# Ten modulation steps of the first FFN: from 32-column matmuls to weighted sums on VectorE

## The chip, the cores and the metric

One core of one Trainium2 chip. The metric is the device time of one launch in microseconds (us); the kernel before took 1458.21 us, the median of three runs.

## The reference

Two transformer blocks of width 1024 on 256 tokens, all in float32. What matters here is the modulation of the first block: from the condition vector c come 6 vectors of 1024 for each layer and 2 for the keys and values, and they shift, scale and gate the activations.

```python
c_act = jax.nn.silu(c)
for l in range(DEPTH):
    shift1, scale1, gate1, shift2, scale2, gate2 = jnp.split(c_act @ ada_w[l] + ada_b[l], 6, axis=-1)
    if l == N_A_LAYERS:
        k_shift, k_scale = jnp.split(c_act @ kv_ada_w + kv_ada_b, 2, axis=-1)
...
    h = modulate(rms_norm(x, norm2_g[l]), shift2, scale2)
    x = x + gate2[:, None, :] * swiglu(h, ffn_w_gate[l], ffn_w_up[l], ffn_w_down[l])
```

So each product is one row of 1024 numbers times a 1024 x 512 block of weights (2 MB), 28 such blocks in all.

## The kernel before

The kernel streams all weights once from HBM. Each engine has its program written out by hand, and semaphores alone tie them; SyncE's queue issues the weight loads in the order in which they will be used.

**The weight stream.** A unit is a block of weights in a ring of four slots (RING): eight k-tiles by 256 columns (1 MB) for gate and up matrices, five or six k-tiles by 256 for the down matrix (DOWN_K, line 40). `take` (line 386) loads unit u when unit u-4 is done (`unit_done`). For the FFNs each unit is split in two parts of reduced width, so that three fast matmuls stand for one of float32: ScalarE casts it (`w_high`, line 594, into PARTS), VectorE subtracts (`w_low`, line 1022, into WL), and TensorE runs the triple in `mm3` (line 1642). All TensorE rows carry line 1610, the helper `mm`.

**The first FFN** (`ffn(0)` in each engine's program; `silu_ffn(0)` on ScalarE). The hidden width of 2816 goes in MT = 11 pairs, each a gate unit and an up unit: 96 matmuls of 128x256 (`gate_up`, line 1719). Behind each pair ScalarE takes the silu (line 614), VectorE multiplies (line 1043), ScalarE and VectorE split the product (lines 625, 1064), and between these they split the next units. Then come the down matrix's 16 units d0 to d15 in four column groups c (`down`, line 1772), 132 matmuls a group. The first group needs the hidden parts; groups 2 and 3 need the two PSUM banks that VectorE read in `down_used` (line 1081), where it also adds the residual and makes the low parts of the units from d4 on.

**The ten modulation steps within it.** 28 blocks of modulation weights are handled as steps s; ten of them (ADA_FFN0, line 42; steps 10 to 19) are done in this FFN, beside its weights. Their loads don't use the ring but an area of their own, ADW, with two halves of 256 columns (`ada_load`, line 396). A step is done by TensorE in two stages:
- `ada_rows` (line 1662), ahead of each pair from the second on: for each of the two halves and eight k-tiles one matmul with 32 copies of the activation CACT as weights. The k-tiles go to four groups of 32 PSUM rows, so that the result is four partial sums in four bands of rows.
- ScalarE copies them to ROWS (`row_copy`, line 684), which has two buffers, s % 2.
- `ada_cols` (line 1685), one pair later: four matmuls with ROWS as weights and a selecting vector (C_SEL) of one column as data. They add the four bands and turn the row of 512 into four columns of 128. ScalarE copies those to MODR.

After the last pair VectorE adds the biases (`modulation`, line 1165) and goes on to `down_used`. Steps 10 and 11 are the gate of this FFN's own output; the other eight serve the layer behind it.

Of the kernel before, what the change touches and what calls it, by code (L numbers as in the profile page):

```python
# [7 lines left out]
SEQ = 256  # L8
# [83 lines left out]
def build(nc, A, out):  # L92
# [4 lines left out]
    with ctx:  # L97
# [113 lines left out]
        ADW, _ = arena(AD_AT, 2, KT * 256)  # L211
        MODR, at = arena(at, 4 * len(ADA_FFN0))
        assert at <= AD_AT
# [104 lines left out]
        def slot(u, kts, cols):  # L318
# [7 lines left out]
            lam_pow b_pow c_pow ct_exp bd_exp k_ready k_used r_ready turn_low s_done gelu_read ada_rows  # L326
            mod_raw scan_ready z_ready meta_used row_copied ada_cols turn_sin turn_cos xt_ready res_ready norm_sq norm_stat norm_std norm_scaled h_ready
# [57 lines left out]
        def _(sp):  # L385
# [10 lines left out]
            def ada_load(n):  # L396

                s = ADA_FFN0[n]
                w, at = (ADA0, s) if s < 12 else (ADA1, s - 12) if s < 24 else (ADA_KV, s - 24)
                if n >= 1:  # L400
                    sp.wait_ge(S["ada_rows"], n)
                for h in range(2):
                    sp.dma_start(ADW[:, h, :].rearrange("p (k c) -> p k c", c=256), w[:, :, at * 512 + h * 256:at * 512 + (h + 1) * 256])\
                        .then_inc(ada_loaded[h], 16)

            u = 0
            while u < len(UNITS):
                if u == 2:
                    sp.dma_start(CN[:, C_LATE:], A["consts"][:, C_LATE:]).then_inc(S["late_loaded"], 16)
                if u == SLOTS:  # L410
# [24 lines left out]

                if kts == "ffn0":
                    for j in range(2):
                        pair(j, j, None)
                    sp.wait_ge(S["y_ready"], KT)
                    ada_load(0)  # L440
                    for j in range(MT):
# [9 lines left out]
                u += 2 * MT  # L451
                with sp.Fori(0, 2) as i:
# [80 lines left out]
        def _(act):  # L533
# [71 lines left out]
            def silu_ffn(f):  # L605
# [3 lines left out]
                def pair(j, p, q, i=None):  # L609
# [16 lines left out]
                    if f == 0 and j < len(ADA_FFN0):  # L626
                        row_copy(ADA_FRONT + j)
                    w_high(u0 + 2 * q + 5, i)

                if f == 0:  # L630
                    for j in range(MT):
                        pair(j, j % 2, j)
                    n = len(ADA_FFN0)
                    act.wait_ge(S["ada_cols"], ADA_FRONT + n)
                    nc.scalar.copy(MODR[:, 4 * n - 4:4 * n], PS[:, 6, 0:4]).then_inc(S["mod_raw"], 1)
                    for d in range(4, 16):
                        w_high(u0 + 2 * MT + d)
                    return
# [45 lines left out]
            def row_copy(s):  # L684

                if s < ADA_FRONT or s >= ADA_LAST:
                    act.wait_ge(S["unit_done"], ada_unit(s) + 2)
                else:
                    act.wait_ge(S["ada_rows"], s - ADA_FRONT + 1)
                if s >= 2:  # L690
                    act.wait_ge(S["ada_cols"], s - 1)
                if ADA_FRONT <= s < ADA_FRONT + len(ADA_FFN0):
                    n = s - ADA_FRONT
                    b = 4 * ((n + 1) % 2) + 2
                    if n >= 1:
                        act.wait_ge(S["ada_cols"], s)
                        nc.scalar.copy(MODR[:, 4 * n - 4:4 * n], PS[:, b, 0:4])
                    src = PS[:, b:b + 2, SEQ:]
                else:
                    src = PS[:, 4 if s < ADA_FRONT else 7, :].rearrange("p (h c) -> p h c", h=2)  # L700
                nc.scalar.copy(ROWS[:, s % 2, :].rearrange("p (h c) -> p h c", h=2), src).then_inc(S["row_copied"], 1)
# [270 lines left out]
        def _(dve):  # L972
# [60 lines left out]

            def ffn(f):
# [284 lines left out]
            dve.wait_ge(S["mod_raw"], 1)  # L1319
            for c0, c1, at in ((40, 48, 0), (96, 112, 8), (48, 64, 24)):  # L1320
                modulation(c0, c1, MODR[:, at:at + c1 - c0])
            gain(2, 48 + ADA_SCALE1, VAT["norm1_g"] + KT)
            link(gain(4, KV_SCALE, VAT["kv_norm_g"]))
            down_used(0, ADA_GATE2)
# [283 lines left out]
        def _(pe):  # L1608
# [53 lines left out]
            def ada_rows(s):  # L1662

                n = s - ADA_FRONT
                ring = s < ADA_FRONT or s >= ADA_LAST
                if s >= 1:
                    pe.wait_ge(S["row_copied"], s if ring else s - 1)
                for h in range(2):
                    if ring:
                        u = ada_unit(s) + h  # L1670
                        loaded(u)
                        w = slot(u, KT, 256)
                    else:
                        pe.wait_ge(ada_loaded[h], 16 * (n + 1))
                        w = ADW[:, h, :].rearrange("p (k c) -> p k c", c=256)
                    b, c0 = (4 if s < ADA_FRONT else 7, h * 256) if ring else (4 * ((n + 1) % 2) + 2 + h, SEQ)
# [3 lines left out]
                    if ring:  # L1680
                        ins.then_inc(S["unit_done"], 1)
                    elif h == 1:
                        ins.then_inc(S["ada_rows"], 1)

            def ada_cols(s):
# [3 lines left out]
                elif s < ADA_LAST:  # L1689
                    b, at = 4 * ((s - ADA_FRONT) % 2) + 2, 0  # L1690
# [4 lines left out]
                pe.wait_ge(S["row_copied"], s + 1)  # L1695
                if s >= 4:
                    pe.wait_ge(S["ada_used"], 1)
                for m in range(4):
                    ins = mm(PS[:, b, at + m:at + m + 1], ROWS[:, s % 2, m * P:(m + 1) * P], CN[:, C_SEL:C_SEL + 1], True, True)
# [15 lines left out]
            def ffn(f):  # L1715
# [3 lines left out]
                def gate_up(j, q, p, i=None, first=None):  # L1719
# [5 lines left out]
                    step = ADA_FRONT + q - 1 if f == 0 and q >= 1 else None  # L1725
                    if step is not None:
                        ada_rows(step)
                        if q >= 2:
                            ada_cols(step - 1)
                    for side in range(2):  # L1730
                        u = u0 + 2 * q + side
                        split(u, i)
                        if side == 1 and step is not None:
                            pe.wait_ge(S["row_copied"], step + 1)
# [34 lines left out]
                if f == 0:  # L1769
                    ada_cols(ADA_FRONT + len(ADA_FFN0) - 1)  # L1770
# [10 lines left out]

                if f == 3:
# [18 lines left out]
                with pe.Fori(0, 2) as i:  # L1801
                    for c in range(2):

                        pe.wait_ge(S["res_ready"], i * 4 + (KT * FFN_OUT[f] + 2 * c - 2))
                        if f == 0 and c == 1:
                            pe.wait_ge(S["mod_raw"], 1)
# [426 lines left out]
```

## Time and profile before

| | |
|---|---|
| Runs | 1457.47, 1458.21, 1459.5 us; median 1458.21 |
| The profiled execution's own time | 1459.93 us |
| Its span, first to last instruction | 1458.1 us |
| Mean granted clock of TensorE | 0.947 of full |
| TensorE busy | 1355.9 us, 93% |
| VectorE busy | 794.5 us, 54% |
| ScalarE busy | 623.6 us, 43% |
| Moved by DMA | 246.89 MB, mean 169 GB/s |

The first FFN runs from 209.4 to about 429.5 us of the span. PE is TensorE's matmuls, PEld its weight loads, DVE VectorE, ACT ScalarE, POOL GpSimd, SPq the issues on SyncE's queue. A row of a timeline gives start, duration, engine, line, operation, what it writes and reads, and the count; in brackets how long the engine was idle before it and who released it. Float32 matmuls are counted as two instructions. A duration of a matmul holds its whole way through the array; the distance of two starts is what one costs in a row of them.

### The profile page before, as it was taken

To read this page: it belongs to the slowest core of one execution; us is meant where nothing else is said; L and a number is where in the kernel's file an instruction comes from. 1 tells how busy PE (TensorE), PEld (TensorE's weight loads), DVE (VectorE), ACT (ScalarE), POOL (GpSimd) and SP (SyncE) were. 2 spreads that over 40 slices of the span, in tenths; PEclk is the share of its full clock that TensorE was granted. 3 is DMA by queue.
4 is the path that set the end of the run, shared out by engine and by line. 5 is a ranking of instruction groups with operands and counts; after the bars stand their busy time and mean duration, and the time that the engine had idled before them with its cause. 6 is when DMAs were issued, how large, how long until landed. Compare 5 with 4: busy or idle time off the path is not lost.

```text
span 1458.1 us, 27052 instructions
## 1 busy us (share of the span) xinstructions
PE 1355.9 (93%) x11784; PEld 1240.8 (85%) x11784; DVE 794.5 (54%) x1040; ACT 623.6 (43%) x810; POOL 86.3 (6%) x79
## 2 busy tenths in 40 slices
PE   5579789999999989899999999999898999899998
PEld 3467689999996445799999999999898889899997
DVE  5953663433443366656655565644645755766543
ACT  4731353333334534454434544434542544644442
POOL 6532300000000011000000000000000000000000
PEclk7658799999999999999999999999999999999999
DMA  9505558987564247256546555456253434355452
GB/s 254 192 2 173 177 174 273 309 285 235 166 210 159 87 147 229 71 162 190 184 152 189 184 176 173 162 166 199 86 165 116 140 117 157 124 181 185 154 181 87
DMA packets 237797, 246.89 MB, mean 169 GB/s; under 512 B 5544, under 2 KB 233336, under 8 KB 237704
## 3 DMA queue, kind: packets, MB, share of 16 engines
q1 hardware_dynamic: 236968, 243.82, 52.2%
q0 software_dynamic: 480, 1.57, 0.6%
q8 instruction: 73, 1.20, 0.3%
q10 hardware_dynamic: 256, 0.14, 0.0%
q14 instruction: 20, 0.16, 0.0%
HBM read 244.47 MB, written 1.05 MB: 168 GB/s over the span
## 4 chain that ended last, share of the span: by engine, by line
PE 84%; DVE 7%; ACT 4%; DMA 2%; issue 1%; POOL 0%; SPq 0%; DVEq 0%; ACTq 0%
PE PS L1610 83%; DMA RING<-in_ada_w 1%; DVE WL L1027 1%; ACT PARTS L599 1%; DMA RING<-in_w_in 1%; DVE ARENA L1394 1%; PE PS L2145 0%; DVE ARENA L1222 0%; DVE ARENA L1219 0%; DVE ARENA L1225 0%; DVE ARENA L1408 0%; DVE ARENA L1224 0%; DVE ARENA L1223 0%; DVE ARENA L1218 0%; ACT ARENA L859 0%
## 5 line engine op out<-in xcount | busy, mean ns | idle before, releaser
L1610 PE MATMUL PS<-PARTS 128*128 128x256 f32 (+3 forms) x3544 | 840.0, 285 | 0.0
L1610 PEld LDWEIGHTS PS<-PARTS 128*128 128x128 f32 (+1 forms) x3544 | 618.7, 191 | 0.6
L1027 DVE TENSOR_TENSOR WL<-RING,PARTS 128x2048 fp32r<-128x2048 f32 (+2 forms) x189 | 387.5, 2054 | 297.0 <-ACT PARTS L599 296.3
L1610 PE MATMUL PS<-HH,WL 128*128 128x256 f32 (+3 forms) x1832 | 527.6, 288 | 17.2 <-DVE PARTS L1016 7.9
L1610 PE MATMUL PS<-HH,PARTS 128*128 128x256 f32 (+3 forms) x1832 | 524.5, 286 | 0.0
L599 ACT CAST PARTS<-RING 128x2048 fp32r<-128x2048 f32 (+2 forms) x189 | 323.5, 1715 | 305.4 <-DMA RING<-in_w_ffn_out 66.9
L1610 PEld LDWEIGHTS PS<-HH,WL 128*128 128x128 f32 (+1 forms) x1832 | 351.1, 192 | 23.7 <-issue 15.6
L1610 PEld LDWEIGHTS PS<-HH,PARTS 128*128 128x128 f32 (+1 forms) x1832 | 350.7, 191 | 0.4
L1610 PE MATMUL PS<-PARTS,WL 128*128 128x256 f32 (+1 forms) x832 | 237.6, 286 | 3.7 <-DVE WL L1027 3.3
L1610 PEld LDWEIGHTS PS<-PARTS,WL 128*128 128x128 f32 x832 | 159.2, 191 | 5.3 <-issue 4.7
L1610 PE MATMUL PS<-ARENA 128*32 128x63 f32 (+5 forms) x720 | 59.8, 277 | 5.6 <-ACT ARENA L874 2.8
L1610 PEld LDWEIGHTS PS<-ARENA 128*32 128x32 f32 (+4 forms) x720 | 35.9, 137 | 25.1 <-issue 14.4
L1610 PEld LDWEIGHTS PS<-H,ARENA 32*128 32x128 f32 (+1 forms) x576 | 35.0, 276 | 12.9 <-issue 8.3
L1610 PE MATMUL PS<-RING,CACT 128*32 128x256 f32 x576 | 44.4, 459 | 1.6 <-DMA RING<-in_ada_w 0.9
L1610 PE MATMUL PS<-H,ARENA 32*128 32x64 f32 (+4 forms) x576 | 37.6, 366 | 8.9 <-ACT ARENA L743 4.3
L1610 PEld LDWEIGHTS PS<-ARENA,RING 128*96 128x96 f32 (+2 forms) x176 | 27.0, 158 | 21.0 <-issue 8.9
L1610 PE MATMUL PS<-ARENA,RING 128*96 128x256 f32 (+2 forms) x176 | 41.2, 382 | 2.4 <-ACT ARENA L811 2.1
L1053 DVE TENSOR_TENSOR SQ<-PS,RSTD 128x512 f32<-128x512 f32 (+1 forms) x33 | 23.1, 699 | 35.5 <-PE PS L1610 35.5
L1610 PEld LDWEIGHTS PS<-CN,ARENA 128*128 128x128 f32 x224 | 30.5, 212 | 12.5 <-issue 9.6
L1610 PE MATMUL PS<-ARENA,CN 96*96 96x512 f32 (+3 forms) x66 | 30.9, 562 | 10.0 <-DVE ARENA L1371 4.4
L1610 PE MATMUL PS<-SQ,CN 128*128 128x256 f32 (+2 forms) x154 | 38.0, 399 | 2.2 <-ACT SQ L549 1.2
L621 ACT ACTIVATE SG<-SG 128x544 f32<-128x544 f32 (+1 forms) x22 | 14.2, 645 | 59.4 <-DVE SG L1049 59.4
(293 smaller groups left out, 1099.1 us busy)
## 6 DMA issues: line engine op xcount, KB each, us to landing
RING<-in_w_ffn_in SPq DMA_DIRECT2D x44, 1024.0 KB, 5.1
RING<-in_ada_w SPq DMA_DIRECT2D x36, 1024.0 KB, 7.0
RING<-in_ffn_w_gate SPq DMA_DIRECT2D x22, 1024.0 KB, 5.4
RING<-in_ffn_w_up SPq DMA_DIRECT2D x22, 1024.0 KB, 5.3
RING<-in_w_in SPq DMA_DIRECT2D x20, 1024.0 KB, 5.3
ARENA<-in_ada_w SPq DMA_DIRECT2D x12, 1024.0 KB, 8.7
RING<-in_ffn_w_down SPq DMA_DIRECT2D x16, 768.0 KB, 4.4
RING<-in_w_ffn_out SPq DMA_DIRECT2D x16, 768.0 KB, 4.2
```

The lines of the kernel that those rows point to most:

```text
L599: nc.scalar.copy(WH[:, u % SLOTS, 0:w], RING[:, u % SLOTS, 0:w]).then_inc(S["w_hi"], 1)
L621: ins = nc.scalar.activation(SG[:, p, :, 0:T], SG[:, p, :, 0:T], ACT.Silu)
L1027: V.tensor_tensor(WL[:, u % SLOTS, 0:w], RING[:, u % SLOTS, 0:w], WH[:, u % SLOTS, 0:w].bitcast(fp32), SUB)\
L1053: V.tensor_tensor(up, PS[:, 4 * p + 2:4 * p + 4, 0:T], by_token, MUL).then_inc(S["up_read"], 1)
L1394: V.scalar_tensor_tensor(v, v, VEC[0:rows, g:g + 1], SDH[0:rows, s1, :], MUL, MUL).then_inc(S["hp_scaled"], 1)
L1610: return nc.tensor.matmul(o, lhsT, rhs, start=start, stop=stop)
```

## The change

The 20 half steps (`ada_sum`, new; numbered 0 to 19) replace `ada_rows` in the FFN: half h of a step holds k-tiles 4h to 4h+3 of all 512 columns. VectorE multiplies each weight tile (128 x 512) by its column of CACT and adds it to the step's buffer in ROWS, four operations in a chain, each waiting for the one before it. So ROWS holds the sum over k-tiles, still spread over 128 partitions, and the four one-column matmuls of `ada_cols` sum over the partitions with a column of ones.

ADW now has eight k-tiles of 512; a load is half a step (1 MB) and waits until the half step two before it is done. Eleven half steps lie in the pairs, ahead of VectorE's wait for silu; nine in the down part, between the low parts of the units. Five steps' columns come ahead of every second pair; two steps' ahead of column group 1, one ahead of groups 2 and 3, and the last ahead of d15. SyncE issues the nine late loads behind d0, d1, d6, d7, d8, d10, d11, d13 and d15. The columns' results stay in PSUM, the copies on ScalarE fall away, and the biases of all but the first two steps are added after the down part. On TensorE and SyncE the down part is written out rather than looped. Of the diff, the core:

```diff
@@ SyncE: ada_load
-                if n >= 1:
-                    sp.wait_ge(S["ada_rows"], n)
-                for h in range(2):
-                    sp.dma_start(ADW[:, h, :].rearrange("p (k c) -> p k c", c=256), w[:, :, at * 512 + h * 256:at * 512 + (h + 1) * 256])\
-                        .then_inc(ada_loaded[h], 16)
+                if n >= 2:
+                    sp.wait_ge(S["ada_sum"], n - 1)
+                sp.dma_start(ADW[:, 4 * h:4 * h + 4, :], w[:, 4 * h:4 * h + 4, at * 512:(at + 1) * 512]).then_inc(ada_loaded[h], 16)
...
                     for j in range(MT):
                         if j + 2 < MT:
                             pair(j + 2, j + 2, None)
-                        if j + 1 < len(ADA_FFN0):
-                            ada_load(j + 1)
+                        if j + 2 <= MT - 1:
+                            ada_load(j + 2)
...
+                    for d in range(16):
+                        k0, k1 = DOWN_K[d % 4], DOWN_K[d % 4 + 1]
+                        take(u + d, slot(u + d, k1 - k0, 256), down[:, k0:k1, d // 4, :])
+                        if d in (0, 1, 6, 7, 8, 10, 11, 13, 15):
+                            ada_load(MT + (0, 1, 6, 7, 8, 10, 11, 13, 15).index(d))
@@ ScalarE: silu_ffn
-                    if f == 0 and j < len(ADA_FFN0):
-                        row_copy(ADA_FRONT + j)
@@ VectorE
+            def ada_sum(n):
+                s, h = n // 2, n % 2
+                acc = ROWS[:, s % 2, :]
+                dve.wait_ge(ada_loaded[h], 16 * (s + 1))
+                if h == 0 and s >= 2:
+                    dve.wait_ge(S["ada_cols"], ADA_FRONT + s - 1)
+                if h == 1:
+                    dve.wait_ge(S["ada_sum"], n)
+                for k in range(4 * h, 4 * h + 4):
+                    if k == 0:
+                        ins = V.tensor_scalar(acc, ADW[:, k, :], CACT[:, k:k + 1], None, MUL)
+                    else:
+                        ins = V.scalar_tensor_tensor(acc, ADW[:, k, :], CACT[:, k:k + 1], acc, MUL, ADD)
+                    if k % 4 < 3:
+                        link(ins)
+                ins.then_inc(S["ada_sum"], 1)
@@ ffn, pair
+                        ada_sum(j)
                         dve.wait_ge(S["silu_ready"], j + (base + 1))
@@ down_used
                             for d in range(4 * c + 4, 4 * c + 7):
                                 w_low(u0 + d)
+                                if f == 0 and (c == 0 or d < 4 * c + 6):
+                                    ada_sum(MT + 2 * c + d - 4 * c - 4 + (c > 0))
+                        elif f == 0:
+                            ada_sum(18)
+                            ada_sum(19)
@@ TensorE: gate_up
-                    step = ADA_FRONT + q - 1 if f == 0 and q >= 1 else None
-                    if step is not None:
-                        ada_rows(step)
-                        if q >= 2:
-                            ada_cols(step - 1)
+                    if f == 0 and q >= 2 and q % 2 == 0:
+                        ada_cols(ADA_FRONT + q // 2 - 1)
@@ down part
+                    for c in range(4):
+                        if c >= 2:
+                            pe.wait_ge(S["res_ready"], KT * R_FFN0 + 2 * c - 2)
+                        for s in ((), (5, 6), (7,), (8,))[c]:
+                            ada_cols(ADA_FRONT + s)
+                        for h in range(4):
+                            if c == 0 and h == 3:
+                                pe.wait_ge(S["hid_lo"], hb + MT)
+                            if c == 3 and h == 3:
+                                ada_cols(ADA_FRONT + 9)
+                            down(c, None, h)
```

In `ada_cols` these steps wait for `ada_sum` at 2 (s - ADA_FRONT) + 2 in place of `row_copied`.

## Rows read from the trace of the kernel before

**Rows 1.** The page: busy shares, and the chain that ended last by engine.

```profile
PE 1355.9 (93%) x11784; PEld 1240.8 (85%) x11784; DVE 794.5 (54%) x1040; ACT 623.6 (43%) x810; POOL 86.3 (6%) x79
...
PE 84%; DVE 7%; ACT 4%; DMA 2%; issue 1%; POOL 0%; SPq 0%; DVEq 0%; ACTq 0%
```

**Rows 2.** Chain of waits in order of time: start us, us, what.

```profile
209.42 223.67 PE PS L1610 x2000
```

**Rows 3.** Groups by form, 209 to 434 us: count, busy us, mean ns, idle.

```profile
L1610 PE MATMUL PS<-ARENA,CACT 128*32 128x256 f32 x320 | 19.3, 382 | 0.0
L1027 DVE TENSOR_TENSOR WL<-RING,PARTS 128x1536 fp32r<-128x1536 f32 x8 | 14.1, 1758 | 20.7 <-ACT PARTS L599 20.7
L1027 DVE TENSOR_TENSOR WL<-RING,PARTS 128x1280 fp32r<-128x1280 f32 x8 | 11.9, 1492 | 8.6 <-ACT PARTS L599 8.6
```

**Rows 4.** Timeline of TensorE about one pair.

```profile
237.66 1.93 PE L1610 MATMUL PS<-ARENA,CACT 128*32 128x256 f32 x32
239.52 1.05 PE L1610 MATMUL PS<-CN,ARENA 128*128 128x1 f32 x8
240.44 0.36 PE L1610 MATMUL PS<-HH,WL 128*128 128x256 f32 x1
...
251.97 0.42 PE L1610 MATMUL PS<-ARENA,CACT 128*32 128x256 f32 x4
```

**Rows 5.** Timeline behind a pair's end: TensorE, SyncE's queue, ScalarE.

```profile
224.25 1.93 PE L1610 MATMUL PS<-ARENA,CACT 128*32 128x256 f32 x32
...
224.35 0.37 SPq L391 DMA_DIRECT2D RING<-in_ffn_w_up  x1
...
229.76 1.91 ACT L599 CAST PARTS<-RING 128x2048 fp32r<-128x2048 f32 x1 [2.01 <-DMA RING<-in_ffn_w_up]
```

**Rows 6.** Timeline of VectorE behind the same pair's end.

```profile
231.70 2.29 DVE L1027 TENSOR_TENSOR WL<-RING,PARTS 128x2048 fp32r<-128x2048 f32 x1 [2.04 <-ACT PARTS L599]
```

**Rows 7.** Groups of VectorE by form, whole span; linked operations among them.

```profile
L1394 DVE SCALAR_TENSOR_TENSOR ARENA<-ARENA,VEC 96x512 f32<-96x512 f32 x8 | 6.5, 870 | 0.7 <-ACT ARENA L859 0.6
L1419 DVE TENSOR_SCALAR ARENA<-ARENA,SMALL 128x256 f32<-128x256 f32 x16 | 5.6, 347 | 0.0
...
L1603 DVE SCALAR_TENSOR_TENSOR ARENA<-PS,RSTD,ARENA 128x512 f32<-128x512 f32 x4 | 2.7, 744 | 1.8 <-ACT RSTD L968 1.8
...
L1336 DVE SCALAR_TENSOR_TENSOR ARENA<-ARENA 32x256 f32<-32x256 f32 x3 | 1.2, 416 | 0.1
...
L1231 DVE TENSOR_SCALAR ARENA<-ARENA 128x2048 f32<-128x2048 f32 x1 | 1.2, 1226 | 0.0
...
441.87 1.31 DVE L1336 SCALAR_TENSOR_TENSOR ARENA<-ARENA 32x256 f32<-32x256 f32 x3
```

**Rows 8.** Timelines, down part: TensorE's start and end, a load, its cast.

```profile
367.20 0.36 PE L1610 MATMUL PS<-PARTS,WL 128*128 128x256 f32 x1
...
429.46 0.81 PE L1610 MATMUL PS<-SQ,CN 128*128 128x256 f32 x3
...
371.87 4.59 SPq L391 DMA_DIRECT2D RING<-in_ffn_w_down  x2
...
376.23 1.48 ACT L599 CAST PARTS<-RING 128x1536 fp32r<-128x1536 f32 x1 [4.07 <-DMA RING<-in_ffn_w_down]
```

**Rows 9.** TensorE behind gaps: timeline, and windows with granted clock (PEclk).

```profile
202.89 0.91 PE L1610 MATMUL PS<-SQ,CN 128*128 128x256 f32 x3 [1.23 <-ACT SQ L549]
...
1218.68 0.39 PE L1610 MATMUL PS<-HH,WL 128*128 128x256 f32 x1 [1.87 <-DVE PARTS L1583]
...
1221.00:1223.00 2.00, 2.00 (x12) 2.00 (x11) 1.77 (x1) 2.00 (x2) 0.00 (x0) 0.51 0.00 0
...
214.00:216.00 2.00, 2.00 (x11) 2.00 (x11) 0.82 (x2) 2.00 (x2) 0.00 (x0) 0.50 0.03 8
```

**Rows 10.** Windows: busy time by engine, PEclk, DMA share, GB/s.

```profile
238.00:252.00 14.00, 14.00 (x140) 13.03 (x133) 5.87 (x4) 5.25 (x6) 0.00 (x0) 1.00 0.97 306
...
370.00:433.00 63.00, 63.00 (x523) 62.31 (x521) 25.38 (x27) 21.73 (x23) 0.00 (x0) 1.00 0.64 202
```

More of the change, by code:

```diff
@@ L210, in build @@
         assert at <= AD_AT
-        ADW, _ = arena(AD_AT, 2, KT * 256)
-        MODR, at = arena(at, 4 * len(ADA_FFN0))
-        assert at <= AD_AT
+        ADW, _ = arena(AD_AT, KT, 512)
         OUTT, _ = arena(AD_AT, 2, D)
@@ L396, in ada_load @@
             def ada_load(n):
[L398 removed]
+                s, h = ADA_FFN0[n // 2], n % 2
                 w, at = (ADA0, s) if s < 12 else (ADA1, s - 12) if s < 24 else (ADA_KV, s - 24)
[L400 to L404 removed]
+                if n >= 2:
+                    sp.wait_ge(S["ada_sum"], n - 1)
+                sp.dma_start(ADW[:, 4 * h:4 * h + 4, :], w[:, 4 * h:4 * h + 4, at * 512:(at + 1) * 512]).then_inc(ada_loaded[h], 16)
             u = 0
@@ L440, in _ @@
                     ada_load(0)
+                    ada_load(1)
                     for j in range(MT):
@@ L451, in _ @@
                 u += 2 * MT
+                if kts == "ffn0":
+                    for d in range(16):
[3 more added lines that the diff above has]
+                            ada_load(MT + (0, 1, 6, 7, 8, 10, 11, 13, 15).index(d))
+                    u += 16
+                    continue
                 with sp.Fori(0, 2) as i:
@@ L632, in silu_ffn @@
                         pair(j, j % 2, j)
-                    n = len(ADA_FFN0)
-                    act.wait_ge(S["ada_cols"], ADA_FRONT + n)
-                    nc.scalar.copy(MODR[:, 4 * n - 4:4 * n], PS[:, 6, 0:4]).then_inc(S["mod_raw"], 1)
                     for d in range(4, 16):
@@ L684, in row_copy @@
             def row_copy(s):
[L686 to L689, printed above, removed]
+                act.wait_ge(S["unit_done"], ada_unit(s) + 2)
                 if s >= 2:
                     act.wait_ge(S["ada_cols"], s - 1)
[L692 to L701, printed above, removed]
+                nc.scalar.copy(ROWS[:, s % 2, :], PS[:, 4 if s < ADA_FRONT else 7, :]).then_inc(S["row_copied"], 1)
             def c_compact():
@@ L1318, in _ @@
             ffn(0)
-            dve.wait_ge(S["mod_raw"], 1)
-            for c0, c1, at in ((40, 48, 0), (96, 112, 8), (48, 64, 24)):
-                modulation(c0, c1, MODR[:, at:at + c1 - c0])
+            dve.wait_ge(S["ada_cols"], ADA_FRONT + 5)
+            modulation(40, 48, PS[:, 2, SEQ:SEQ + 8])
+            down_used(0, ADA_GATE2)
+            dve.wait_ge(S["ada_cols"], ADA_LAST)
+            for c0, c1, at in ((96, 112, 8), (48, 64, 24)):
+                modulation(c0, c1, PS[:, 2, SEQ + at:SEQ + at + c1 - c0])
             gain(2, 48 + ADA_SCALE1, VAT["norm1_g"] + KT)
             link(gain(4, KV_SCALE, VAT["kv_norm_g"]))
-            down_used(0, ADA_GATE2)
             rstd(2)
@@ L1662, in ada_rows @@
             def ada_rows(s):
-                n = s - ADA_FRONT
-                ring = s < ADA_FRONT or s >= ADA_LAST
                 if s >= 1:
-                    pe.wait_ge(S["row_copied"], s if ring else s - 1)
+                    pe.wait_ge(S["row_copied"], s if s < ADA_FRONT else s - len(ADA_FFN0))
                 for h in range(2):
[L1669 to L1676, printed above, removed]
+                    u = ada_unit(s) + h
+                    loaded(u)
+                    w = slot(u, KT, 256)
+                    b, c0 = 4 if s < ADA_FRONT else 7, h * 256
                     for k in range(KT):
@@ L1679, in ada_rows @@
                         ins = mm(PS[g, b, c0:c0 + 256], CACT[:, k:k + 1].broadcast_to([P, 32]), w[:, k, :], k < 4, k >= 4)
[L1680 to L1683, printed above, removed]
+                    ins.then_inc(S["unit_done"], 1)
             def ada_cols(s):
@@ L1689, in ada_cols @@
                 elif s < ADA_LAST:
-                    b, at = 4 * ((s - ADA_FRONT) % 2) + 2, 0
+                    b, at = 2, SEQ + 4 * (s - ADA_FRONT)
                 elif s < ADA_LAST + 2:
@@ L1694, in ada_cols @@
                     b, at = 2, 384 + 4 * (s - ADA_LAST - 2)
-                pe.wait_ge(S["row_copied"], s + 1)
+                from_sums = ADA_FRONT <= s < ADA_LAST
+                if from_sums:
+                    pe.wait_ge(S["ada_sum"], 2 * (s - ADA_FRONT) + 2)
+                else:
+                    pe.wait_ge(S["row_copied"], s + 1 if s < ADA_FRONT else s + 1 - len(ADA_FFN0))
                 if s >= 4:
                     pe.wait_ge(S["ada_used"], 1)
+                pick = one if from_sums else CN[:, C_SEL:C_SEL + 1]
                 for m in range(4):
-                    ins = mm(PS[:, b, at + m:at + m + 1], ROWS[:, s % 2, m * P:(m + 1) * P], CN[:, C_SEL:C_SEL + 1], True, True)
+                    ins = mm(PS[:, b, at + m:at + m + 1], ROWS[:, s % 2, m * P:(m + 1) * P], pick, True, True)
                 ins.then_inc(S["ada_cols"], 1)
@@ L1732, in gate_up @@
                         split(u, i)
-                        if side == 1 and step is not None:
-                            pe.wait_ge(S["row_copied"], step + 1)
                         if f >= 1 and isinstance(j, int) and j == 1 and side == 1:
@@ L1780, in down @@
                     ins.then_inc(S["unit_done"], 1)
+                if f == 0:
+                    for c in range(4):
[9 more added lines that the diff above has]
+                            down(c, None, h)
+                    return
                 if f == 3:
@@ L1804, in ffn @@
                         pe.wait_ge(S["res_ready"], i * 4 + (KT * FFN_OUT[f] + 2 * c - 2))
-                        if f == 0 and c == 1:
-                            pe.wait_ge(S["mod_raw"], 1)
                         for h in range(4):
```

6 lines of the change are left out of this document (2 added, 4 removed).

## The prediction

> **What bounds the kernel now.** I read the page first: its shares of the span and its chain that ended last [rows 1]. TensorE is busy 93% of the span and holds 84% of the chain; VectorE is busy 54%. So the question is what the first FFN looks like. The chain in order of time shows it [rows 2]: from 209.42 to 433.09 us there is one piece of 223.67 us, TensorE and nothing else. Every microsecond of matmul taken out there is a microsecond of the span, and every microsecond that TensorE is made to wait there is one too. No other engine has yet stood in its way.
>
> The groups of that stretch [rows 3] give what the ten modulation steps cost TensorE: 320 short matmuls on CACT, 32 a step. The timeline of one pair [rows 4] gives the price of a step: the 32 start at 237.66, the eight one-column matmuls at 239.52, the next pair's matmuls at 240.44, the next step at 251.97. So rows 1.86 us, columns 0.92 us, and 96 matmuls of a pair with its switches 11.53 us.
>
> VectorE and ScalarE have gaps in each pair, but they lie where a fixed sequence leaves them [rows 5, 6]. A pair ends at E = 224.25 (start of the 32 short ones behind it, [rows 5]). The next up block is then issued at 224.35, its cast starts at 229.76, VectorE's low part runs from 231.70 to 233.99, that is to E + 9.75. There VectorE is idle until the next silu.
>
> **The change, part by part.**
>
> *Removed.* Ten times 32 short matmuls: 10 x 1.86 = 18.6 us off TensorE's path. Some switches between kinds go too: a pair takes 11.53 us where 96 matmuls at 0.118 make 11.34, and five of the ten pairs now follow their neighbour with no other kind between: 5 x 0.14 = 0.7 us. ScalarE's row copies (0.59 us) and MODR copies go; they hung on TensorE and nobody on the path waited for them, so nothing. The columns stay, 0.92 us each, five in the pairs, five in the down part: nothing in the sum.
>
> *Added on VectorE.* Twenty half steps, each four linked operations on 128x512. SCALAR_TENSOR_TENSOR of that size took 0.744 us, three linked ones on 32x256 took 1.31 us from first start to last end at 0.416 each, so the link adds 0.03: I take 0.775. The first of an even half step is a TENSOR_SCALAR: 0.347 us for 256 elements and 1.227 for 2048 give 0.47 for 512, 0.50 with its link [rows 7]. An even half step is 0.50 + 3 x 0.775 = 2.83 us, an odd one 3.10 us, all of them 59 us. Bounds of the operation: 0.45 us if it ran at TENSOR_SCALAR's pace, 0.87 us as the 96x512 form with a pointer took [rows 7]. The row of its own size decides. (The Trainium skill, "VectorE: DVE Perf Modes", section on the TRN2 errata, gives 58 cycles plus one an element for an operation from SBUF, which makes 0.59 us here as an estimate; the 0.744 us speaks against it. By the page the whole change would come to about +9 us in place of the sum below, still a loss.)
>
> *In the pairs.* Half step j stands ahead of the wait for pair j's silu, behind pair j-1's second low part. It starts at E + 9.75 and an odd one ends at E + 12.9. TensorE, without the 1.86 us, is through the next pair at E + 11.5 and stands before the columns, which need that half step. They come before every second pair: five waits of 1.2 to 1.4 us, 6.5 us. VectorE's multiplication also comes later, which costs nothing: TensorE needs it a pair later.
>
> *SyncE's queue.* A pair's loads go from 4 blocks of 1 MB to 3. But a half step's load waits for the half step two before it, and weight blocks stand behind it. In the pairs it is free at once. In the down part it is not: the load of half step 11 waits for half step 9 (E9 + 1.2), d1's block goes out behind it only at E9 + 1.6 and lands at E9 + 9.1; a block of 1.05 MB lands 5.3 us after its issue, 3.3 us of them its turn (0.97 share and 306 GB/s in [rows 10]) and 2.0 latency, and one in front adds up to 3.3: 1.2 + 2.0 + 3.3 + 2.5 for d1's 0.79 MB is this 9.1. Cast, low part and half step 10 then end 1.5 us after the down part starts, at E9 + 13.6.
>
> *In the down part* (its start is 0; units of 4.28 and 3.57 us, 15.7 us a column group: 528 matmuls from 367.20 to 429.46 [rows 8]). A down block lands in 4.4 us when nothing is ahead, its cast takes 1.4 (1.2 for the smaller blocks, by size), its low part 1.7 for 1536 and 1.4 for 1280 elements [rows 3, 8].
> - Load 12 goes out at 1.5, when half step 10 is done, and d2 behind it lands at 8.9; cast to 10.1, low part to 11.6. TensorE is there at 8.6: a wait of 3.1 us.
> - Group 1 begins with the columns of steps 5 and 6, so it needs half step 13. On VectorE stand, in this order, d4's low part, 11, d5's, 12, d6's, 13: 1.7 + 3.1 + 1.7 + 2.8 + 1.4 + 3.1 = 13.8 us. d4, the last of load 12, d2, d3 and d4 one after the other (1.5 + 2.0 + 3.3 + 2.1 + 2.1 + 2.5), lands at 13.5 and is cast by 14.9, so the row ends at 28.8. TensorE is there at 18.8: waits of 0.9 and 8.1 us about the first columns. With no late load at all it would be 4.3 + 4.5 + 1.4 + 13.8 = 24.0 against 15.7, so most of this wait doesn't hang on the queue.
> - Group 2 needs half step 15. From the group's start: d8's block to 8.8, cast 10.2, low part 11.9, half step 14 to 14.8; d9's block, behind load 15, to 14.6, cast 16.1, low part 17.8, half step 15 to 20.9. TensorE is there at 15.7: 5.2 us.
> - Group 3 needs 17: 8.8, 10.3, 12.0, half step 16 to 14.8, d13's low part 16.5, half step 17 to 19.6: 3.9 us. The last columns wait 0.5 us for half step 19.
>
> Together 21.7 us of waits in the down part.
>
> *The clock.* TensorE is at the full level throughout this stretch after 216 us. Elsewhere a gap of 1.87 us ahead of 1218.68 was followed by about half the clock, still 0.51 in the stretch up to 1223 us, some 3.6 us in all, and after the wait before this FFN it was 0.50 from 209.42 until 216, 6.6 us [rows 2, 9]. Half of such a stretch is lost: 1.8 and 3.3 us. I take 2.3, nearer to the first, whose gap also lies in dense work. Four long waits make 9.2 us; but of the 2.3 us after the first, the second wait takes up the most, as half step 13 is no later for it, which leaves about 6.5 us. Bounds: 0 (the gaps are too few) and 10. The waits of 1.3 us in the pairs I leave at the full clock, as the gap of 1.23 us ahead of 202.89 was [rows 9].
>
> *The end.* Final modulation sums move behind the down part, about 1 us of VectorE, under TensorE's stat matmuls and ScalarE's std. The next weights (kva) need the slot of d12 and land before the longer down part ends. Nothing.
>
> **Sum.** -18.6 - 0.7 + 6.5 + 21.7 + 6.5 = +15.4 us. The profiled execution took 1459.93 us (span 1458.1); 1475.3 on that, and 1.7 us less against the runs' median of 1458.21: **1473.5 us**.
>
> **Rivals.**
> - *VectorE hides the sums.* If the operation ran at about 0.45 us, a half step would be 1.7 to 1.8 us, the waits in the pairs would go, and those of the down part would shrink to 2.1, 6.0, 3.9 and 2.4 us: -18.6 - 0.7 + 14.4 = -4.9, 1453.3 us, if these gaps leave the clock alone. It decides at about 0.57 us an operation, a half step of 2.2 us. For it: VectorE is busy only 25 of 63 us there [rows 10]. Against it: every row of SCALAR_TENSOR_TENSOR. With the clock's price added this lands within 0.2% of before. 8% faster, 5% no change.
> - *The waits come, the clock stays.* The clock's 6.5 us don't come: 1467 us. For it: TensorE works densely between the gaps. Against it: [rows 9]. 17%.
> - *The stream gets tight.* In the pairs the DMA share was 0.97 at 306 GB/s, in the down part 0.64 at 202 [rows 10]. Seven more blocks of 1 MB at 3.3 us are 23 us on 40 us of busy in a stretch of 63: nearly full. If a block takes 3.6 us, each weight block comes later where a half step's load is ahead, some 0.3 us in each pair's wait and 0.7 to 1 us in each of the down part's: +4 us, 1477.5, and 1480 and more with slower VectorE operations. 14%.
> - My forecast, 56%.
>
> **How the numbers follow.** A measurement of this kernel tells about 0.2% (2.9 us) from no change, so faster is below 1455.3, slower above 1461.1. Faster 0.08, same 0.05, slower 0.87. The range: down to 1460, which takes the second rival and an operation of 0.6 us with a cheap clock; up to 1483, an operation of 0.87 us and the tight stream together.
>
> **What would show it.** On VectorE twenty groups of four operations, 0.74 us each. In the pairs, TensorE waits for ARENA from VectorE, 1.3 us, before every second pair only, and pairs of about 11.4 us. In the down part, four gaps, the longest near 8 us and named after the same VectorE line, the first named after WL; granted clock 0.5 behind them. SyncE's down loads bunched behind a half step's load. The FFN ends near 445 us in place of 430. I am wrong if the gaps are absent or under 2 us, if the half step takes 2.2 us or less, or if the time beyond the gates shrinks.

## The result and the profile after

The changed kernel took 1483.1 us (median of six runs, 1479.38 to 1486.08), the kernel before 1458.86 us beside it: ratio 1.0172, 95% interval 1.0148 to 1.0196. It is slower, as forecast, but 9.6 us more so than the 1473.5 us, and 0.1 us beyond the upper end of the range. The profiled execution took 1483.5 us, its span is 1481.6 us against 1458.1.

The page of the changed kernel, busy shares and the chain by engine; they answer to [rows 1].

```profile
PE 1349.2 (91%) x11464; PEld 1244.9 (84%) x11464; DVE 849.0 (57%) x1120; ACT 617.4 (42%) x790; POOL 86.3 (6%) x79
...
PE 80%; DVE 9%; ACT 5%; DMA 3%; issue 3%; POOL 0%; SPq 0%; DVEq 0%; ACTq 0%
```

320 matmuls are gone, and TensorE's busy time fell by only 6.7 us, although [rows 3] and [rows 4] gave them 18.6. Something else made the rest of its work longer. The chain in order of time (start us, us, what) answers to the one piece of 223.67 us in [rows 2].

```profile
233.86 1.48 issue
235.34 26.91 PE PS L1624 x200
262.24 1.53 issue
263.77 23.81 PE PS L1624 x200
287.58 1.36 issue
288.95 25.34 PE PS L1624 x200
314.28 1.67 issue
315.95 25.38 PE PS L1624 x200
341.33 1.82 issue
343.15 18.25 PE PS L1624 x140
...
382.87 19.69 PE PS L1624 x140
402.56 5.14 issue
407.70 19.25 PE PS L1624 x140
426.95 3.90 issue
430.85 23.96 PE PS L1624 x164
...
456.99 19.21 PE PS L1624 x80
```

Two things are to be seen. The gaps: five before the columns in the pairs, 7.86 us together, and in the down part 5.14 and 3.90 us before groups 2 and 3. The view names no releaser for them ("issue"), but three of them can be followed to VectorE: they end 0.10 us behind the last operation of the half step that is asked for. In the pairs half step 1 ends at 232.13 + 3.11 = 235.24 and TensorE goes on at 235.34; before groups 2 and 3 VectorE ends at 407.60 and 430.75, TensorE goes on at 407.70 and 430.85. And the pieces between them: each piece of 200 matmuls is the same work (eight one-column matmuls and two pairs), but one takes 23.81 us, two some 25.35 and one 26.91. The windows (us; busy time and count on PE, PEld, DVE, ACT, POOL; granted clock, DMA share, GB/s) say why.

```profile
237.00:239.00 2.00, 2.00 (x11) 2.00 (x11) 2.00 (x2) 0.00 (x0) 0.00 (x0) 0.50 1.09 339
...
264.00:266.00 2.00, 2.00 (x19) 2.00 (x19) 1.57 (x2) 1.19 (x2) 0.00 (x0) 1.00 1.01 348
...
291.00:293.00 2.00, 2.00 (x11) 2.00 (x11) 2.00 (x2) 0.02 (x1) 0.00 (x0) 0.50 1.05 353
...
382.90:387.00 4.10, 4.10 (x19) 4.10 (x20) 2.11 (x3) 0.00 (x0) 0.00 (x0) 0.50 0.14 51
...
457.00:460.00 3.00, 3.00 (x9) 2.41 (x10) 3.00 (x9) 3.00 (x9) 0.00 (x0) 0.62 0.02 5
```

The granted clock fell to half, the 1.2 GHz level, behind four of the five short gaps (0.50 again from 318 us and 0.51 from 345 us): 11 matmuls in 2 us in place of 19. Only the piece of 23.81 us stayed at 1.00. Before, the clock held 1.00 all through this stretch [rows 10]. The other three short waits and the long one of the down part are in TensorE's timeline, each named in brackets.

```profile
366.42 0.39 PE L1624 MATMUL PS<-PARTS,WL 128*128 128x256 f32 x1 [0.82 <-DVE WL L1015]
...
374.02 1.05 PE L1624 MATMUL PS<-CN,ARENA 128*128 128x1 f32 x8 [0.26 <-DVE ARENA L1035]
...
382.87 1.44 PE L1624 MATMUL PS<-CN,ARENA 128*128 128x1 f32 x6 [7.80 <-DVE ARENA L1035]
```

VectorE's side: the groups of the first FFN by form, and the timeline of one odd half step (232.13) and one even (243.25, 243.76). They answer to [rows 7].

```profile
L1035 DVE SCALAR_TENSOR_TENSOR ARENA<-ARENA,CACT 128x512 f32<-128x512 f32 x70 | 52.6, 751 | 2.2
...
L1033 DVE TENSOR_SCALAR ARENA<-ARENA,CACT 128x512 f32<-128x512 f32 x10 | 4.8, 480 | 0.0
```

```profile
232.13 3.11 DVE L1035 SCALAR_TENSOR_TENSOR ARENA<-ARENA,CACT 128x512 f32<-128x512 f32 x4
235.15 0.68 DVE L1050 TENSOR_TENSOR SG<-SG,PS 128x512 f32<-128x512 f32 x1
...
243.25 0.48 DVE L1033 TENSOR_SCALAR ARENA<-ARENA,CACT 128x512 f32<-128x512 f32 x1
243.76 2.33 DVE L1035 SCALAR_TENSOR_TENSOR ARENA<-ARENA,CACT 128x512 f32<-128x512 f32 x3
```

**Where the 23.5 us of span come from.** At the full clock a piece of 200 is 23.81 us and the last one of the pairs 16.74 (a run below shows it), so the clock took 3.1, 0, 1.5, 1.6 and 1.5 us: 7.7 us in the pairs. In the down part a group with its eight column matmuls is 15.7 + 0.9 = 16.6 us at the full clock; the pieces of 19.69 and 19.25 us lost 3.1 and 2.6, and the last, with its two sets of columns and the 3.6 us of matmuls behind it, some 2.8: 8.5 us. The waits there are 0.82 + 0.26 + 7.80 + 5.14 + 3.90 = 17.9 us. So -19.3 (removed) + 7.9 + 7.7 + 17.9 + 8.5 = +22.7. What stands behind the FFN began at 455.86 us in place of 434.07, +21.8, and the FFN itself 0.7 us earlier (its first matmul at 208.72 in place of 209.42), so it is 22.5 us longer; the sum agrees within 1 us. Another 1.7 us is the clock once more: the first 80 matmuls behind the FFN take 19.21 us in place of 17.52, with a clock of 0.62 at 457 us, though the gap ahead of them, 2.2 us, was there before too.

```profile
435.20 17.52 PE PS L1610 x80
```

That is the row of the kernel before. Its 17.52 us stands alone: the same 80 matmuls take 19.13 to 19.21 us in the traces of all eleven other kernels here, also in the one that is the kernel before with some matmuls left out. So these 1.7 us can't be put down to the change; one trace of each kernel doesn't tell more.

### The profile page after: what moved, and what is told of

It reads as the page before. It is cut to its first block, busy times and chain, and to the rows that moved or that the text cites. A ratio compares the mean times of both kernels' runs of the same rounds, so it can differ in the third digit from the quotient of the medians.

```text
span 1481.6 us, 26386 instructions
## 1 busy us (share of the span) xinstructions
PE 1349.2 (91%) x11464; PEld 1244.9 (84%) x11464; DVE 849.0 (57%) x1120; ACT 617.4 (42%) x790; POOL 86.3 (6%) x79
## 4 chain that ended last, share of the span: by engine, by line
PE 80%; DVE 9%; ACT 5%; DMA 3%; issue 3%; POOL 0%; SPq 0%; DVEq 0%; ACTq 0%
PE PS L1624 79%; DVE WL L1015 2%; DMA RING<-in_ada_w 1%; ACT PARTS L604 1%; DMA RING<-in_w_in 1%; DVE ARENA L1408 1%; DVE ARENA L1035 1%; DMA RING<-in_ffn_w_gate 0%; DMA RING<-in_ffn_w_down 0%; PE PS L2159 0%; DVE ARENA L1234 0%; DVE ARENA L1237 0%; DVE ARENA L1231 0%; DVE ARENA L1230 0%; DVE ARENA L1236 0%
## 5 line engine op out<-in xcount | busy, mean ns | idle before, releaser
L1624 PE MATMUL PS<-PARTS 128*128 128x256 f32 (+3 forms) x3544 | 848.8, 288 | 0.0
L1624 PEld LDWEIGHTS PS<-PARTS 128*128 128x128 f32 (+1 forms) x3544 | 627.0, 194 | 0.6
L1624 PEld LDWEIGHTS PS<-HH,WL 128*128 128x128 f32 (+1 forms) x1832 | 355.0, 194 | 24.5 <-issue 15.9
L1624 PE MATMUL PS<-PARTS,WL 128*128 128x256 f32 (+1 forms) x832 | 240.7, 289 | 4.6 <-DVE WL L1015 4.1
L1624 PEld LDWEIGHTS PS<-PARTS,WL 128*128 128x128 f32 x832 | 162.4, 195 | 6.3 <-issue 4.7
L1624 PE MATMUL PS<-CN,ARENA 128*128 128x1 f32 x224 | 33.6, 272 | 30.3 <-issue 16.9
L1035 DVE SCALAR_TENSOR_TENSOR ARENA<-ARENA,CACT 128x512 f32<-128x512 f32 x70 | 52.6, 751 | 2.2
```

The source lines that it names most:

```text
L1035: ins = V.scalar_tensor_tensor(acc, ADW[:, k, :], CACT[:, k:k + 1], acc, MUL, ADD)
L1624: return nc.tensor.matmul(o, lhsT, rhs, start=start, stop=stop)
```

## The experiments

Ratios are against the kernel before, run beside each. Its median was 1458.86 us beside the kernels of the removed half, of the operation left out and the two with both orders together; 1460.15 beside those with one and two operations more; 1455.79 beside the other four. On that scale the changed kernel is 1.0172. Each trace is of one execution, and the stages ahead of this FFN, the same in the changed kernel and in all that are made from it, end at different times: its first matmul starts at 204.86 us in one and at 210.51 in another. So where spans of two kernels differ by a few microseconds, the length from that first matmul to the first one behind the FFN is the better measure: 225.78 us before, 248.27 in the changed kernel.

### The price of what was removed

The kernel before, without the row matmuls of k-tiles 4 to 7, so without half of the modulation products of these ten steps (the start and stop flags go with it).

```diff
-                    for k in range(KT):
+                    for k in range(KT if ring else 4):
```

> The kernel before, with the second half of each of the ten modulation steps' row matmuls left out (k-tiles 4 to 7, so the sums of these steps are half sums); all loads, copies and columns stay. It measures the term for what the change takes off TensorE: by my price of 1.86 us a step, half of ten steps is 9.3 us, so 1449 us against 1458 in the median, if nothing else then binds. If the loads of 4 MB a pair bind in its place, less: each pair could not go under about 13.4 us, and then it would be near 1451 us or above, with waits for weights in the pairs.

Ratio 0.9960 (0.9940 to 0.9980), span 1451.1 us. The chain, against [rows 2]:

```profile
209.59 214.99 PE PS L1610 x1840
```

8.7 us less for 160 of the 320 matmuls, where half of 18.6 is 9.3, and no wait for weights in the pairs. The removed term was sized rightly, within some 1.2 us of the whole. The time fell by less, 5.8 us by the ratio (2.9 to 8.8): in the trace 1.7 of the 8.7 us go to the 80 matmuls behind the FFN, 19.21 us in place of 17.52.

### The gaps in the pairs: taken away, made shorter, made longer

First, the columns moved between the gate and the up unit of the same pair, 5.7 us later, when the half step has long ended.

```diff
-                    if f == 0 and q >= 2 and q % 2 == 0:
-                        ada_cols(ADA_FRONT + q // 2 - 1)
                     for side in range(2):
+                        if f == 0 and q >= 2 and q % 2 == 0 and side == 1:
+                            ada_cols(ADA_FRONT + q // 2 - 1)
```

> The changed kernel, with the columns in the pairs put between the gate and the up unit of the same pair, 5.7 us later, so that half steps 1, 3, 5, 7 and 9 are done when TensorE comes. My theory (the short waits also cost clock): the five waits of 1.4 to 1.8 us go, 7.9 us, and with them the stretches at half clock behind four of them, 7.7 us, which makes 15.6 us in the pairs; some 3 us come back as a longer wait ahead of d2, since half step 10 is no earlier. About 1470 us, granted clock 1.00 through all pairs. Rival (the half clock in the pairs comes from something else, VectorE's sums or the fuller DMA stream beside TensorE): only the waits go, the clock still falls to 0.5 in several pairs, about 1477 us.

1471.4 us (four runs), ratio 1.0108 (1.0077 to 1.0140). Its window over the pairs, then its waits from 340 to 450 us (engine, line, what for: us, times, longest):

```profile
216.00:348.00 132.00, 131.29 (x1114) 131.09 (x1113) 89.07 (x86) 48.33 (x41) 0.00 (x0) 1.00 0.72 244
```

```profile
PE PS L1624 <- issue: 10.5, 2, 6.6
PE PS L1624 <- DVE WL L1015: 7.6, 1, 7.6
PE PS L1624 <- DVE ARENA L1035: 7.3, 1, 7.3
```

No gap and no loss of clock in the pairs, with VectorE's sums and the stream as they were: all 15.6 us of the two came back there. Some 9 us of them reached the time (7.6 in the FFN of the trace, 240.71 us), because the down part starts earlier and meets a longer wait for d2's low part, 7.6 us in place of 0.82, and one of 6.6 in place of 5.1. The wait for d2 is the queue's, below.

Then the length. The last operation of each odd half step in the pairs left out (k-tile 7 is missing from these sums):

```diff
-                for k in range(4 * h, 4 * h + 4):
+                last = 4 * h + (3 if n < MT and h == 1 else 4) - 1
+                for k in range(4 * h, last + 1):
```

> The changed kernel, with the last operation of the odd half steps in the pairs left out (k-tile 7 of steps 1 to 5), which brings the half step's end 0.78 us forward, so that TensorE's gap ahead of the columns is some 0.7 us in place of 1.4 to 1.8. If a gap of this size leaves the clock alone: the waits shrink by 4 us and the 7.7 us of half clock go, minus some 2 us that come back ahead of d2, about 1473 us. If any gap there brings the clock down in most pairs: only the 4 us, about 1479 us.

1471.62 us (three runs), ratio 1.0089 (1.0059 to 1.0119). Its chain in the pairs, and a window over them:

```profile
230.39 0.73 issue
231.12 23.85 PE PS L1625 x200
...
328.39 1.11 issue
329.50 16.74 PE PS L1625 x140
```

```profile
216.00:348.00 132.00, 128.25 (x1079) 127.38 (x1078) 84.08 (x79) 48.12 (x41) 0.00 (x0) 1.00 0.73 243
```

Gaps of 0.48 to 1.11 us are left, and the clock is 1.00 throughout. The other direction: one and two operations more in each of the same half steps (k-tile 7 is added two and three times).

```diff
+                extra = 1 if n < MT and h == 1 else 0
+                for i in range(4 + extra):
+                    k = 4 * h + min(i, 3)
```

> The changed kernel, with a fifth operation in the odd half steps within the pairs (the last k-tile is added twice), so that each is 0.78 us longer. The gaps of TensorE before the columns in the pairs should come out at 2.1 to 2.6 us in place of 1.4 to 1.8. Theory A, the clock's loss hangs on a gap and not on its length: a double pair behind a gap, 23.8 us at the full clock, takes 25.4 us behind each of the five (one step of 1.5 us lost), the first FFN is longer by the gaps alone, 5 x 0.8 = 4 us: span about 1486, ratio 1.020. Theory B, the loss grows with the gap: double pairs of 26.9 us and more behind each, another 5 to 8 us, span 1491 to 1494.

> As the one with five operations, with six in each odd half step of the pairs: gaps of 2.9 to 3.4 us. Theory A: double pairs of 25.4 us, gaps 5 x 1.6 = 8 us longer than the changed kernel's, span about 1490. Theory B: double pairs of 27 us and more, span 1498 and above.

1488.77 us (two runs), ratio 1.0197 (1.0168 to 1.0227), span 1485.6; and 1494.64 us (two runs), ratio 1.0237 (1.0204 to 1.0270), span 1490.9. The chain of the second, in the pairs:

```profile
231.50 2.84 issue
234.34 26.91 PE PS L1626 x200
261.25 3.08 issue
264.32 25.37 PE PS L1626 x200
```

Both spans are those of theory A (1486 and 1490), but partly by luck: these two executions began the FFN 1.3 and 2.8 us earlier than the changed kernel's. From its first matmul on, the FFN is 5.5 and 12.0 us longer than there, where A had 4 and 8 and B at least 9 and 16. The gaps in the pairs add up to 7.9, 12.3 and 15.4 us in the three kernels, the clock's loss behind them to 7.7, 9.3 and 12.2 us. So neither theory holds as it stands: a loss comes in steps of about 1.5 us, as in A, but behind longer gaps two steps came more often, though twice the gap did not make twice the loss. All gaps of this place, from seven kernels:

| Gaps in the pairs, us | Kernels | Gaps | without loss | about 1.5 us | about 3 us |
|---|---|---|---|---|---|
| 0.48 to 1.11 | last operation left out | 5 | 5 | 0 | 0 |
| 1.15 to 2.43 | changed kernel and the three of the next part | 20 | 4 | 14 | 2 |
| 2.16 to 3.14 | one operation more | 5 | 0 | 4 | 1 |
| 2.77 to 3.67 | two operations more | 5 | 0 | 2 | 3 |

The loss is the length of the piece behind the gap less 23.81 us (16.74 for the last); the smaller losses are 1.5 to 1.6 us, the larger 2.8 to 3.1. Within the second row the length doesn't decide: 1.38 and 1.53 us cost nothing in one place, 1.18 and 1.20 cost 1.5 in others.

### The waits of the down part: VectorE's row of work, or SyncE's queue

Late half steps cut to one operation each (k-tiles 1 to 3 and 5 to 7 are missing in the last nine half steps):

```diff
-                for k in range(4 * h, 4 * h + 4):
+                for k in range(4 * h, 4 * h + (4 if n < MT else 1)):
```

> The changed kernel, with the nine half steps of the down part cut to their first operation; the other three operations of each, that is k-tiles 1 to 3 and 5 to 7, are left out of the sums of steps 5.5 to 10. All loads and waits stay. Theory A (VectorE's row of work is what TensorE waits for): the three long waits shrink from 7.8, 5.1 and 3.9 to about 4, 3 and 1.5 us, and the run is some 9 to 10 us shorter than the changed kernel, about 1473 us. Theory B (the loads behind one another on SyncE's queue set the waits): they stay within 1 us of what they were, about 1480 us.

1471.79 us (three runs), ratio 1.0106 (1.0073 to 1.0138). The long wait is 4.7 us in place of 7.8, those before groups 2 and 3 are 2.87 and 1.35 in place of 5.14 and 3.90, near theory A's 4, 3 and 1.5. Work taken off VectorE shortens each of them. What is left of the long one now hangs on a modulation load, which its chain shows just ahead of the half step's one operation:

```profile
368.89 7.30 DMA ARENA<-in_ada_w
```

So with this little work on VectorE the transfer is next in line.

The nine late loads left out, and with them the waits for them (the sums of these half steps use whatever the buffer still holds):

```diff
-                        if d in (0, 1, 6, 7, 8, 10, 11, 13, 15):
-                            ada_load(MT + (0, 1, 6, 7, 8, 10, 11, 13, 15).index(d))
...
-                dve.wait_ge(ada_loaded[h], 16 * (s + 1))
+                if n < MT:
+                    dve.wait_ge(ada_loaded[h], 16 * (s + 1))
```

> The changed kernel, with the nine loads of the down part and the waits for them left out; VectorE's nine half steps work on the blocks that lie there, so steps 5.5 to 10 are computed from old weights. Theory A (VectorE's row of work): the wait ahead of d2 goes and that of group 2 shrinks by about 1 us, but 7.6 us ahead of group 1 and 4 ahead of group 3 stay: some 4 to 5 us shorter than the changed kernel, about 1478 us. Theory B (the queue): the long waits fall under 2 us each, 20 us shorter, about 1463 us.

1476.89 us (two runs), ratio 1.0153 (1.0113 to 1.0193). With nothing but weight blocks in the queue, the waits before the columns are still 7.6, 4.65 and 3.93 us:

```profile
396.59 4.65 issue
...
420.24 3.93 issue
```

So they are VectorE's row of work, four operations after each low part, and not the modulation loads. (The FFN is 4.8 us shorter than the changed kernel's, as theory A had it; the ratio alone doesn't part this kernel from the changed one.) Then TensorE's order: the columns of these five steps placed later, in the down part's units, with VectorE and the queue as they were.

```diff
-                        for s in ((), (5, 6), (7,), (8,))[c]:
-                            ada_cols(ADA_FRONT + s)
                         for h in range(4):
...
-                            if c == 3 and h == 3:
-                                ada_cols(ADA_FRONT + 9)
+                            if (c, h) in ((1, 2), (2, 0), (2, 2), (3, 2)):
+                                ada_cols(ADA_FRONT + {(1, 2): 5, (2, 0): 6, (2, 2): 7, (3, 2): 8}[c, h])
                             down(c, None, h)
+                    ada_cols(ADA_FRONT + 9)
```

> The changed kernel, with only TensorE's order in the down part changed: the columns of step 5 come ahead of d6, of step 6 ahead of group 2, of step 7 ahead of d10, of step 8 ahead of d14 and of step 9 behind d15, so that VectorE may be late with a half step while TensorE still has units to do. By my timetable the waits for sums ahead of the groups go and short ones for low parts of weight blocks (1 to 2 us, ahead of d11 and d13) stay: 18 us shorter than the changed kernel, about 1464 us, the pairs as before. If the waits only move on to the low parts of the weights (VectorE as a whole too slow for the down part), less than 8 us is won.

1462.41 us (six runs), ratio 1.0041 (1.0016 to 1.0066). The waits for the sums are gone from the down part; what is left there stands before low parts, and its longest is 4.7 us where 1 to 2 were expected:

```profile
PE PS L1624 <- DVE WL L1015: 7.8, 4, 4.7
```

About 19 of the 22.5 us that the FFN had grown by are regained by order alone (229.07 us in place of 248.27), with VectorE's new work untouched, 57 us in the whole FFN.

### Both orders, then the queue

The two moves of columns together:

> Both moves of the columns together, that of the pairs and that of the down part, all else as in the changed kernel. My theory (the two losses lie in different places and add): 1483 less 11.6 (what the first gave) less 20.7 (what the second gave) would be 1451 us; the longer wait ahead of d2 that the first brings stays, and VectorE's work in the down part now lies tighter, so 1450 to 1456 us, within 0.5% of the kernel before. Rival (VectorE's work of the down part is the bound once the pairs are shorter): 1460 us or more, with TensorE waiting for low parts in every group.

1456.9 us (ten runs), ratio 0.9987 (0.9965 to 1.0010), level with before and 1 us above what was expected. TensorE now waits 13.9 us for low parts in the down part, 7.1 of them before d2. The issues on SyncE's queue show the cause: the loads from d2 on stand behind half step 12's load of 346.38, and that one had to wait for VectorE's half step 10.

```profile
346.38 0.37 SPq L400 DMA_DIRECT2D ARENA<-in_ada_w  x1
346.79 17.31 SPq L389 DMA_DIRECT2D RING<-in_ffn_w_down  x5
```

So last, the same with the late loads issued further back in the queue, behind d1, d3, d6, d7, d9, d11, d13, d14 and d15:

```diff
-                        if d in (0, 1, 6, 7, 8, 10, 11, 13, 15):
-                            ada_load(MT + (0, 1, 6, 7, 8, 10, 11, 13, 15).index(d))
+                        if d in (1, 3, 6, 7, 9, 11, 13, 14, 15):
+                            ada_load(MT + (1, 3, 6, 7, 9, 11, 13, 14, 15).index(d))
```

> As the one with both moves, and the nine late loads behind d1, d3, d6, d7, d9, d11, d13, d14 and d15 instead of d0, d1, d6, d7, d8, d10, d11, d13 and d15, so that no weight block stands behind a load whose half step is not yet free. Theory (what is left of the loss is weight blocks held up in SyncE's queue, above all d2): the wait ahead of d2 goes, the down part has waits of 1 to 3 us in all, the clock stays at full level in it, and the run is 10 to 14 us shorter than the one with both moves: about 1440 us, faster than the kernel before by 1%. Rival (VectorE's 57 us of work in a part of 67 us can't be placed without waits): 1450 us or more.

1447.61 us (six runs, 1437.92 to 1449.15), ratio 0.9906 (0.9875 to 0.9936): faster than both kernels. It is 9.3 us below the one with both moves, where 10 to 14 were expected, and 7 us above the 1440 us. Its waits for VectorE's sums and low parts in the FFN, two pieces of its chain, and two rows of SyncE's queue:

```profile
PE PS L1624 <- DVE ARENA L1035: 1.0, 1, 1.0
PE PS L1624 <- DVE WL L1015: 0.9, 1, 0.9
```

```profile
214.38 132.09 PE PS L1624 x1117
...
418.68 19.15 PE PS L1624 x80
```

```profile
335.69 6.90 SPq L389 DMA_DIRECT2D RING<-in_ffn_w_down  x2
342.64 0.53 SPq L400 DMA_DIRECT2D ARENA<-in_ada_w  x1
```

The wait before d2 has gone, the loads of d2 and d3 (335.69) now being ahead of half step 12's (342.64). From its first matmul on the FFN takes 208.17 us, 17.6 less than in the kernel before: most of the 19.3 us that were taken out. The span gained 12.2 of these. The FFN began 1.1 us later here, and the next 80 matmuls take 19.15 us in place of 17.52; the other 2.7 us lie in the stages behind and are open. All nine late loads were moved at once, so how much of the gain is d2's alone isn't shown.

## Why the prediction was wrong in size, by its own steps

- **The sign and its reason were right.** TensorE alone was the path, the removed matmuls were worth their 18.6 us within some 1.2 us (shown by the kernel with half of them), and the order of the columns turned VectorE's new work into waits (shown by moving the columns: the waits went, the work stayed).
- **Half steps.** Forecast 2.83 and 3.10 us at 0.744 + 0.03 an operation; measured 2.8 (243.25 to the end of the last) and 3.0 (232.13 to the next start at 235.15), 0.751 us an operation. Right, and the row of its own size was the one to take. That ruled out the rival in which VectorE hides the sums. The estimate of 0.59 us from the Trainium skill, "VectorE: DVE Perf Modes", section on the TRN2 errata, is not what was measured.
- **The waits in the pairs.** 6.5 us forecast, 7.86 measured (1.36 to 1.82 each). Slightly low: the prediction's own marks, E + 12.9 and E + 11.5, leave 1.4 us, and 1.3 went into the sum.
- **The waits in the down part.** 3.1, 0.9, 8.1, 5.2 and 3.9 us forecast; 0.82, 0.26, 7.80, 5.14 and 3.90 measured. The last three within 0.3 us, and it was VectorE's row of work, as argued. The first was too high: half step 12's load went out at 356.49, 0.5 us before the down part began at 356.96, where 1.5 us behind it was forecast. The last pair ran partly at half clock, which gave the queue time; in the kernel with shorter gaps and no loss of clock in the pairs this wait was 2.3 us. In the kernel without gaps it was 7.6 us: there the queue's cost was more than I had priced. The 15.7 us taken for a column group are 15.6 by the rows (62.26 us for four, [rows 8]), too little to matter.
- **The step that failed** is this: "The waits of 1.3 us in the pairs I leave at the full clock, as the gap of 1.23 us ahead of 202.89 was." One gap in another stretch was taken for a rule. Four of five such gaps brought the clock to half, 7.7 us; with the gaps shortened to 1.11 us and less or taken away the loss went, with longer ones it came every time. The clock behind the long waits was 8.5 us for 6.5 forecast. So the clock cost 16.2 us in the FFN, forecast 6.5: 9.7 us too little, against waits 2.4 us less than forecast. With the 1.7 us behind the FFN, which were not in the sum, and the 0.7 us by which it began earlier, that makes 8.3 us; the span grew by 8.1 more than the sum of 15.4. That is the miss. The measured median is 9.6 us above the forecast.
- **The stream gets tight:** with no late load at all the waits for sums stayed and the ratio was 1.0153 (1.0113 to 1.0193), so transfers were at most a small part there. In the pairs the stream did lengthen the waits a little: the up block's cast ahead of the five half steps starts 5.45, 5.49, 5.33, 5.63 and 5.79 us after the block's issue (5.41 in [rows 5]), and the waits of 1.48, 1.53, 1.36, 1.67 and 1.82 us follow it one for one, 0.1 us more on average and 0.4 at most, where the rival had 0.3 in each. It fell as the cause, although its 1477.5 us lay nearer to the measured time.
- **The clock stays** fell outright: 0.50 behind each of the three long waits.

## What to carry to other kernels

Price a wait of the engine that bounds the kernel at its length plus what the clock takes behind it; here a wait of 1.4 us cost about as much again, and those of at most 1.1 us nothing but themselves. Where work moves from the bounding engine to another, first move the point at which its result is asked for to where the result is surely there: the same work cost +1.7% with its columns before a pair and -0.9% with them a few microseconds later and the loads behind the weights they had held up. On SyncE's queue here a load that had to wait for a semaphore held up the weight blocks behind it (issued at 346.79 us, behind the load of 346.38 that had waited for half step 10), so it belongs behind the block that is needed first.

## What the runs showed of the hardware

In dense matmul work gaps of 0.48 to 1.11 us left TensorE's clock at the 2.4 GHz level (5 of 5); gaps of 1.15 to 2.43 us brought it to the 1.2 GHz level behind 16 of 20, and gaps of 2.16 to 3.67 us in the two kernels with added operations behind 10 of 10. A loss was 1.5 to 1.6 us or 2.8 to 3.1 us, never between, and not in proportion to the gap; the larger one came behind 2 of 20, 1 of 5 and 3 of 5 gaps of the table's last three rows. (The Trainium skill, "TensorE: Matmul & The Clock Gate", section "What's actually happening", has the slow clock as the state that sustained activity lifts; the granted clock of 0.50 behind these gaps, and of 1.00 again later in the same piece of dense work, agrees.) Why 4 of the 20 stayed at the full level is open. So is why the same gap of 2.2 us behind the FFN was followed by 17.52 us for 80 matmuls in the kernel before and by 19.13 to 19.21 us in the eleven others.
